# Prompt's gated linear attention: the lower levels of each chunk's score matrix as products of 32x32 diagonal blocks

## The reference, cut to what matters

```python
def step(S, inp):                       # one chunk
    qc, kc, vc, lac = inp
    cb = jnp.cumsum(lac, axis=1)        # log decay, for every key channel of its own
    decay = jnp.exp(jnp.where(causal, cb[:, :, None] - cb[:, None, :], -jnp.inf))
    a = jnp.einsum('btshk,bshk->bhts', qc[:, :, None] * decay, kc)
    o = jnp.einsum('bthk,bhkv->bthv', qc * jnp.exp(cb), S) + jnp.einsum('bhts,bshv->bthv', a, vc)
    cl = cb[:, -1]
    S_new = jnp.exp(cl)[..., None] * S + jnp.einsum('bshk,bshv->bhkv', kc * jnp.exp(cl[:, None] - cb), vc)
    return S_new, o
```

## Time and profile before

| | before |
|---|---|
| median of 3 runs | 2766.84 us (2765.65 to 2769.8) |
| the profiled execution's own time | 2768.57 us |
| its span in the profile | 2766.7 us |
| TensorE's mean granted clock | 0.995 |
| PE busy in the whole span | 98% |
| one chunk of the prompt's GLA in the steady state | 14.16 us |

### The profile page before, as it was taken

One profiled execution on the slowest core, in us unless ns is written; L12 is line 12 of the kernel. 1 busy time (PEld: TensorE's weight loads), 2 busy tenths in 40 slices (PEclk: granted clock), 3 DMA queues, 4 the chain that ended last, 5 costly groups with the idle time before them and its releaser, 6 DMA issues.

```text
span 2766.7 us, 44096 instructions
## 1 busy us (share of the span) xinstructions
PE 2704.3 (98%) x17358; PEld 2479.6 (90%) x17358; DVE 1619.5 (59%) x2131; ACT 1051.6 (38%) x1681; POOL 1338.4 (48%) x764
## 2 busy tenths in 40 slices
PE   8999999989999999999999999999999999999998
PEld 8999988788889988999899989998888999889997
DVE  6943237674676677666743410198367666776665
ACT  5552347463533233323333311365252332333233
POOL 4343455343465565565632131287256555555552
PEclk9999999999999999999999999999999999999999
DMA  6477330235565445554342131034384654445541
GB/s 214 158 249 264 138 129 2 81 119 174 155 234 216 163 151 179 208 203 162 144 146 113 46 137 42 16 115 140 135 245 151 224 215 156 162 167 208 215 172 77
DMA packets 212593, 430.65 MB, mean 156 GB/s; under 512 B 27285, under 2 KB 153585, under 8 KB 201972
## 3 DMA queue, kind: packets, MB, share of 16 engines
q1 hardware_dynamic: 203840, 394.92, 40.7%
q0 software_dynamic: 7776, 31.24, 3.0%
q10 hardware_dynamic: 852, 2.75, 0.3%
HBM read 357.89 MB, written 70.94 MB: 155 GB/s over the span
## 4 chain that ended last, share of the span: by engine, by line
PE 64%; DVE 5%; DMA 3%; issue 2%; POOL 2%; ACT 2%; PEld 0%; PEldq 0%; DVEq 0%; ACTq 0%; SPq 0%; POOLq 0%
PE ps L959 24%; PE ps L1037 22%; PE ps L577 7%; PE ps L638 5%; PE ps L1119 4%; DVE units L4189 1%; DMA units_r<-operands 1%; POOL units_r L718 1%; DMA raw<-w_out 1%; PE ps L3073 0%; ACT ps L3630 0%; DVE spare L4194 0%; POOL split L724 0%; DVE lend L4177 0%; DVE spare L784 0%
## 5 line engine op out<-in xcount | busy, mean ns | idle before, releaser
L1332 POOL TENSOR_TENSOR split<-raw,split 128x1024 fp32r<-128x1024 f32 x218 | 562.0, 2589 | 508.5 <-ACT split L1170 482.9
L959 PE MATMUL ps<-units_r,split 128*128 128x288 f32 x5376 | 720.2, 295 | 12.1 <-POOL split L1332 5.4
L959 PEld LDWEIGHTS ps<-units_r,split 128*128 128x128 f32 x5376 | 717.2, 188 | 15.5 <-POOL split L1332 5.8
L1170 ACT ACTIVATE split<-raw 128x1024 fp32r<-128x1024 f32 x218 | 228.4, 1056 | 465.0 <-PE ps L959 176.9
L1447 DVE TENSOR_TENSOR units<-units,ps 128x512 f32<-128x512 f32 x434 | 285.1, 683 | 121.1 <-PE ps L1037 121.1
L577 PE MATMUL ps<-units_r,split 128*128 128x384 f32 x1872 | 330.4, 336 | 2.3 <-POOL split L290 1.5
L577 PEld LDWEIGHTS ps<-units_r,split 128*128 128x128 f32 x1872 | 326.0, 189 | 3.5 <-issue 1.7
L1037 PE MATMUL ps<-split,units_r 128*128 128x512 f32 x1344 | 309.8, 389 | 0.6 <-DVE units L1447 0.6
L1037 PEld LDWEIGHTS ps<-split,units_r 128*128 128x128 f32 x1344 | 252.0, 188 | 53.9 <-DVE units L1447 1.4
L1037 PE MATMUL ps<-split,spare_r 128*128 128x512 f32 x1008 | 235.6, 389 | 0.0
L1037 PEld LDWEIGHTS ps<-split,spare_r 128*128 128x128 f32 x1008 | 188.5, 188 | 38.5
(11 more groups left out here) (535 smaller groups left out, 4052.3 us busy)
## 6 DMA issues: line engine op xcount, KB each, us to landing
units_r<-operands SPq DMA_DIRECT2D x76, 2304.0 KB, 8.8
raw<-w_ff SPq DMA_DIRECT2D x128, 512.0 KB, 4.3
units_r<-operands SPq DMA_DIRECT2D x22, 1152.0 KB, 7.5
raw<-w_in_even SPq DMA_DIRECT2D x14, 1024.0 KB, 9.3
raw<-w_in_odd SPq DMA_DIRECT2D x12, 1024.0 KB, 5.3
operands<-units_r SPq DMA_DIRECT2D x10, 1152.0 KB, 5.6
operands<-units_r SPq DMA_DIRECT2D x22, 512.0 KB, 3.9
operands<-split SPq DMA_DIRECT2D x18, 512.0 KB, 4.0
```

The costliest lines, as they stand in the source:

```text
L959: last = pe.matmul(ps[:, bank + f, 0:HN], right_slot(base, slot, a)[:, COLS * k + P * f:COLS * k + P * (f + 1)], x[:, b, k, HN * g:HN * (g ...
L1170: act.activation(right_slot(base, slot, 0), src, ACT.Copy).then_inc(hi_ready, 1)
L1332: pool.tensor_tensor(right_slot(base, slot, 1), src, right_slot(base, slot, 0), ALU.subtract).then_inc(lo_ready, 1)
```

## The change

Positions of levels 2 to 7 that matter all lie in the four 32x32 diagonal blocks of the chunk's 128x128 matrix. The change computes only these blocks. For such a level PE makes, for each head, four products with 32 stationary columns and 32 moving columns (contraction over all 128 channels) and writes them to PSUM partitions 0-31, 32-63, 64-95 and 96-127, side by side in the same 32 columns: 128x128 for four heads in place of 128x512. DVE chooses them by a 128x128 predicated copy into a small matrix `LA_BLOCKS`, and after the last level four copies of 32 partitions put the blocks into `LA`. Level 0 becomes one product of 64x64 for each head and a plain copy of 64 partitions; level 1 becomes two 32x32 products for each head and two plain copies. The masks of levels 2 to 7 are rewritten to the packed form. `LA` and `LA_BLOCKS` are zeroed once for the prompt and once for the streams' chunk, which goes the same way.

```diff
+        LEVEL_BLOCKS = ((), (0, 2)) + ((0, 1, 2, 3),) * 6
+        LA_BLOCKS = FKST[:, 0:GH * 32].rearrange("p (h t) -> p h t", h=GH)
+        def block_bank(e):
+            return ps[:, e % 4, 0:GH * 32].rearrange("p (h t) -> p h t", h=GH)
...
                 ring_ready(e)
-                out = ring_bank(e)
+                out = ring_bank(e) if l == 0 else block_bank(e)
                 for h in range(GH):
-                    if l == 7:
-                        last = pe.matmul(out[:, h], GKT[:, h, t], GQ[:, h, t], start=True, stop=True)
-                    else:
-                        last = pe.matmul(out[:, h], levels_in(n)[:, l, h], levels_in(n)[:, l, h], start=True, stop=True)
+                    keys, queries = (GKT[:, h, t], GQ[:, h, t]) if l == 7 else (levels_in(n)[:, l, h],) * 2
+                    if l == 0:
+                        last = pe.matmul(out[0:64, h, 64:P], keys[:, 0:64], queries[:, 64:P], start=True, stop=True)
+                    for g in LEVEL_BLOCKS[l]:
+                        rows = slice(32 * g, 32 * g + 32)
+                        columns_ = slice(32 * g + 32 * (l == 1), 32 * g + 32 * (l == 1) + 32)
+                        last = pe.matmul(out[rows, h], keys[:, rows], queries[:, columns_], start=True, stop=True)
                 last.then_inc(l_a, 1)
...
-                dve.copy_predicated(LA, LEVEL_MASK[:, l].unsqueeze(1).broadcast_to([P, GH, P]), ring_bank(e)).then_inc(l_free, 1)
+                if l == 0:
+                    dve.tensor_copy(LA[0:64, :, 64:P], ring_bank(e)[0:64, :, 64:P]).then_inc(l_free, 1)
+                    return
+                if l == 1:
+                    for g in LEVEL_BLOCKS[1]:
+                        rows, columns_ = slice(32 * g, 32 * g + 32), slice(32 * g + 32, 32 * g + 64)
+                        last = dve.tensor_copy(LA[rows, :, columns_], block_bank(e)[rows])
+                    last.then_inc(l_free, 1)
+                    return
+                chosen = dve.copy_predicated(LA_BLOCKS, LEVEL_MASK[:, l, 0:32].unsqueeze(1).broadcast_to([P, GH, 32]), block_bank(e))
+                if l < 7:
+                    chosen.then_inc(l_free, 1)
+                    return
+                after(chosen)
+                for g in range(4):
+                    rows = slice(32 * g, 32 * g + 32)
+                    last = dve.tensor_copy(LA[rows, :, rows], LA_BLOCKS[rows])
+                last.then_inc(l_free, 1)
```

More of the change, by code:

```diff
@@ L69, in constants @@
     gmask[:, 7] = np.eye(P)
+    for i in range(2, 8):
+        gmask[:, i, 0:32] = np.concatenate([gmask[g:g + 32, i, g:g + 32] for g in range(0, P, 32)])
+        gmask[:, i, 32:] = 0
     later = np.zeros((P, 3, 384), np.float32)
@@ L4202, in gla_mix @@
                     dve.tensor_tensor(v, v, ring_bank(e), ALU.mult).then_inc(l_free, 1)
+            dve.memset(LA_BLOCKS, 0.0)
             after(dve.memset(LA, 0.0))
```

## The result

The changed kernel takes **2791.25 us** (median of 4 runs, 2788.49 to 2795.41); the kernel before took 2767.32 in the runs beside it (2765.65 to 2769.80). The ratio is 1.0084, with a 95% interval of 1.0072 to 1.0096: 0.8% slower, where 0.3% faster was forecast, and outside the range. The profiled execution took 2788.83, its span is 2787.0, 20.3 above that of before.

What follows compares the result with a forecast made beforehand. PE (13.87 us) and DVE (13.35) were both taken to nearly fill a turn of 14.16. Each turn was to fall to 12.80, seven times 1.36 giving 9.5 us and 2757.3 us, with a range of 2752 to 2775.

Steps and rivals of the forecast that it cites:

- c = 0.35: PE's time in us for one level of 16 products of 32x32, 0.89 before; bounds considered from 0.21 to 1.12.
- the switch 0.09: On PE, changing between full-width and strip products was priced at some 0.09 us.
- the update starts at 8.25: PE's update, after level 6, was to start 8.25 us after the mix, in place of 10.03.
- The fills' price: DVE's four SBUF-to-SBUF copies after choose 7: 0.218 us each, started 0.15 apart; with choose 7, 1.05 until the mix.
- 12.80: Forecast length in us of one turn, from mix to mix of a chunk, in place of 14.16: 1.36 less.
- The clock: Rival: TensorE's clock falls to 1.2 GHz over the update; 2769 in every turn, 2763 in half; 1 in 10.
- The rival by issuing: PE's issuing sets the level's time: 0.92 us gives 2769, the skill's floor of 0.80 gives 2766; 2 in 10.
- levels 0 to 6: DVE's chooses of these levels were to take 3.16 us together in place of 5.69.
- the sum: Seven turns at 1.36 us give 9.5 us; nothing more from the first chunk or behind the last output.
- Slower: Chance of 0.16 that the kernel loses more than 0.2%, 5.5 us, by no overlap or a clock that stays low.
- no overlap: Rival: short strip products on PE don't overlap, 1.12 us a level, turn 15.30, time 2775; 1 in 10.
- a clock that stays low: The slower part of the clock rival: a third of its 1 in 10, slower than 2763.

Runs made afterwards that it cites:

- e8: The changed kernel with ACT's four squares of the norm replaced by one small square (norm wrong, its cost gone): 2779.71 us, ratio 1.0044.
- e10: e7 with ACT's copy of the turned keys moved behind the second exponential of the next chunk: 2756.18 us, ratio 0.9953 to the kernel before.
- e1: The changed kernel with unread full-width products put into PE's three waits in each chunk: 2792.01 us, ratio 1.0083 to the kernel before.
- e5: The changed kernel with DVE's two products for the streams' keys reading the turned keys from PSUM, not SBUF: 2785.68 us, ratio 1.0068.
- e9: The changed kernel with 64x64 blocks in place of 32x32 and nothing else: 2775.11 us, ratio 1.0019 to the kernel before.
- e7: The changed kernel with 64x64 blocks, fills on ACT, level 7 and its choose before update and state, streams' keys from PSUM: 2762.53 us, ratio 0.9979.
- e11: e7 with eight more unread 32x32 products behind each of levels 1 to 6: 2773.41 us, ratio 1.0019 to the kernel before.

## Why the prediction was wrong, by its own steps

- **The step that failed:** "It takes c = 0.35, the switch 0.09, and the update starts at 8.25." It starts at 9.90, since the update also waits for ACT's norm. The prediction named ACT as setting the pace only behind the last output, and took ACT's end in a turn from no row. Of the 1.78 us forecast at the update (10.03 to 8.25) 0.13 came. e8, with a short norm, and e10, with the norm 0.6 earlier, moved the update as this reading has it. What the change adds behind the update stays: choose 7 and the fills take 1.28 in place of 0.62. A turn at full clock whose fills find POOL idle (the last) is thus 14.75, 0.6 longer, 3.5 us over six turns.
- **The fills' price** is the second term that failed. The prediction has four copies of 0.218 that start 0.15 apart, 0.67 in all, whatever POOL does. They last 0.218 each, but start 0.23 apart: 0.91 with POOL idle, and two to four times that beside it. At full clock every turn but the last pays 1.77 (e1, e5), and with the update nearly as early as was forecast they take 2.84 (e8, update at 8.51). So 12.80 would not have come in those turns even with a short norm.
- **The clock**, a rival at 1 in 10: the granted clock stood at 0.50 for part of five of the six turns, and the update took up to 3.75. The mechanism was named and its chance was too low. Five turns whose fills meet POOL at full clock would cost 4.3 us above those 3.5; what the low clock adds to that is the last 4.0. (3.5, 4.3 and 4.0 make the 11.4 with 0.4 off for a turn of 14.53 that the kernel before had. The split is worked out from the turns of 14.75 and 15.61; at low clock itself the fills take 0.91.) e1's filler and e9's larger blocks each removed the fall from most turns; whether PE's new wait for the norm or its smaller work brings it isn't told apart.
- **PE's pace:** c came out right. Two levels together (64 instructions) take 0.87 at 1840.46, so up to 0.44 a level with its switch, as forecast, and at most 13.6 ns an instruction. The rival by issuing, with its floor of 0.80 a level, is refuted, and with it, for such side-by-side products, the 25 ns of "TensorE: Matmul & The Clock Gate" in the Trainium skill. But a limit of issuing did exist elsewhere: not each instruction's pace but the supply of them. No rival had it.
- **DVE:** choose 0.30 (forecast 0.345), level 1 0.58, levels 0 to 6 3.1 (3.16): right. Outside the turns the sum had nothing, and that failed too. The streams' part lost 6.3 us, of which e5 gives back 5.6, through an instruction that the change did not touch and only shifted. The first chunk lost 2.0, where PE stops for 2.61 and the fills take 1.95, and the streams' chunk 2.2.
- **Slower** had 0.16, from two mechanisms: no overlap, which was refuted, and a clock that stays low, which is 4 of the 20 us. (A tenth for the first and a third of a tenth for the second make 0.13, not 0.16.)

Of e10's 11.2 us of span below the kernel before, by the marks of the first table, 7.5 lie in the six turns, 1.4 ahead of the first mix and 2.0 behind the last of them, while the streams' part is 0.8 longer and the start 0.6 later. The rest takes 834.7 in place of 836.6. No run explains these 1.9; over all the profiled executions that stretch, where nothing was changed, takes 834.6 to 838.2. Blocks of 32x32 with level 7's instructions spread out were not tried.

## What to carry to other kernels

Before crediting a shorter path, list every wait of the instruction at its end, with the time at which each was met before: here a limit 0.3 us under the bound showed no wait in the profile and took back all beyond it. Splitting a product into many small ones is paid for in instructions too: take the largest block that still removes the work (64x64 gave 16 us over 32x32). And a copy between two places in SBUF on VectorE has two prices, by what GpSimd does at that moment; put it on ScalarE or read from PSUM, or fix its place, and check what an earlier or later step now meets.

## What the runs showed of the hardware

- Products of 128 rows by 32x32 on four strips took at most 13.6 ns for each instruction (64 in 0.87 us, the changed kernel); the same with 64x64 on two strips, 64 instructions in 2.28 us, start 33 ns apart (e7).
- Stops marked "issue" of 0.2 to 4.9 us on PE (most after some 190 such small instructions in one chunk), while the instruction queue's packets doubled (7 to 14); 39 of 40 ended 1.2 to 1.6 us after a packet's end. None occurred at 112 instructions for these levels. The Trainium skill ("Runtime: NRT & Kernel Launch", section "Instruction fetch mechanics") holds fetching to be hidden behind the pace of issuing; here it wasn't.
- Fills from SBUF to SBUF took 0.91 with POOL idle, 1.77, 2.84 or 3.33 beside it (four of 32x128), and 0.59 with POOL idle, 0.93 or 2.43 beside it (two of 64x256); the pair of scalar products took 0.88, 5.14 and 6.25 from SBUF, 1.40 from PSUM with POOL beside it.
- A lower granted clock followed one of the two stops of e11, where PE had more work than in e7; in the changed kernel it fell in five turns without a stop.
